# The last layer norm of a one-core decoder step: weight and offset rows in accumulator banks, the shift as a two-scalar form, and the moments of three row tiles on ScalarE

## The reference, cut to what matters

```
def _layer_norm(x, g, b):
    xf = x.astype(jnp.float32)
    mu = jnp.mean(xf, axis=-1, keepdims=True)
    var = jnp.mean(jnp.square(xf - mu), axis=-1, keepdims=True)
    return ((xf - mu) * lax.rsqrt(var + EPS) * g.astype(jnp.float32) + b.astype(jnp.float32)).astype(x.dtype)
...
        x = _layer_norm(DEEPNORM_ALPHA * x + ffn, ln2_g[l], ln2_b[l])
```

## Time and profile before

| | us |
|---|---|
| median of three runs (1813.81 to 1816.19) | 1814.46 |
| the profiled execution's own time | 1814.07 |
| its span in the trace | 1812.3 |
| last stage: first load issued | 1765.42 |
| last stage: first tile there, VectorE starts on it | 1769.18 |
| last stage: last VectorE instruction starts, 1.23 long | 1807.98 |
| last stage: last three stores (tiles 6, 7, 8) issued in a row from | 1805.75 |

### The profile page before, as it was taken

One profiled execution on the slowest core, in us unless ns is written; L12 is line 12 of the kernel. 1 busy time (PEld: TensorE's weight loads), 2 busy tenths in 40 slices (PEclk: granted clock), 3 DMA queues, 4 the chain that ended last, 5 costly groups with the idle time before them and its releaser, 6 DMA issues. The chain is left out here.

```text
span 1812.3 us, 18129 instructions
## 1 busy us (share of the span) xinstructions
PE 1639.4 (90%) x6288; PEld 993.8 (55%) x6288; DVE 526.2 (29%) x1115; ACT 394.0 (22%) x1000; POOL 301.0 (17%) x244
## 2 busy tenths in 40 slices
PE   8999999989889999999986399999999999999950
PEld 7666666656656777777763244444444444444420
DVE  1344444322153445554432500000000000000008
ACT  1211111131034444443420011111111111111102
POOL 0000000021033244443310001111111111111106
PEclk8899999988899999999996599999999999999985
DMA  6132222251343222212112479999999999999935
GB/s 238 37 97 73 75 74 77 59 163 37 110 162 120 82 89 81 94 54 81 53 40 78 161 247 322 325 325 326 321 325 325 329 317 323 326 325 326 321 79 196
DMA packets 177492, 325.83 MB, mean 180 GB/s; under 512 B 43432, under 2 KB 73048, under 8 KB 176152
## 3 DMA queue, kind: packets, MB, share of 16 engines
q1 hardware_dynamic: 166776, 294.30, 46.9%
q0 software_dynamic: 9504, 26.23, 6.2%
q10 hardware_dynamic: 1152, 4.52, 0.6%
HBM read 281.33 MB, written 52.07 MB: 184 GB/s over the span
## 5 line engine op out<-in xcount | busy, mean ns | idle before, releaser
L2075 PE MATMUL bank<-sb_arena 128*128 128x512 f32 x1024 | 451.9, 594 | 2.6 <-ACT sb_arena L2120 2.6
L377 PE MATMUL bank<-sb_arena 128*128 128x368 f32 x1056 | 331.8, 477 | 6.8 <-DMA sb_arena<-xT 6.8
L2075 PEld LDWEIGHTS bank<-sb_arena 128*128 128x128 f32 x1024 | 192.7, 191 | 233.4 <-issue 230.2
L377 PEld LDWEIGHTS bank<-sb_arena 128*128 128x128 f32 x1056 | 202.7, 192 | 133.8 <-DMA sb_arena<-w_conv 6.8
L2091 PE MATMUL bank<-sb_arena 128*128 128x512 f32 x512 | 226.9, 596 | 8.4 <-DMA sb_arena<-w 8.4
L2174 DVE TENSOR_SCALAR sb_oidx<-sb_slot 128x1 int32 x32 | 4.9, 154 | 548.5 <-DMA d_acc<-sb_arena,sb_oidx 548.4
L2091 PEld LDWEIGHTS bank<-sb_arena 128*128 128x128 f32 x512 | 95.5, 192 | 116.9 <-issue 108.2
L2048 POOL DMA_INDIRECT d_acc<-sb_arena,sb_oidx x32 | 51.0, 1592 | 609.0 <-ACT sb_arena L2138 609.0
L941 PE MATMUL bank<-sb_arena 128*128 128x512 f32 (+1 forms) x288 | 133.9, 606 | 6.3 <-DVE sb_rlog L1545 5.0
L742 PE MATMUL bank<-sb_arena 128*128 128x384 f32 (+1 forms) x288 | 100.9, 504 | 8.5 <-DVE sb_arena L1561 8.5
L2120 ACT ACTIVATE sb_arena<-bank 128x512 f32<-128x512 f32 x66 | 35.9, 596 | 266.5 <-PE bank L2069 266.5
(11 more groups left out here) (321 smaller groups left out, 1713.7 us busy)
## 6 DMA issues: line engine op xcount, KB each, us to landing
sb_arena<-w SPq DMA_DIRECT2D x192, 1024.0 KB, 7.9
sb_arena<-w_conv SPq DMA_DIRECT2D x28, 512.0 KB, 4.9
sb_arena<-d_conv SPq DMA_DIRECT2D x7, 1792.0 KB, 7.3
d_conv<-sb_arena SPq DMA_DIRECT2D x22, 512.0 KB, 3.3
sb_arena<-d_gam SPq DMA_DIRECT2D x8, 768.0 KB, 4.1
d_x<-sb_arena SPq DMA_DIRECT2D x9, 512.0 KB, 2.6
sb_arena<-xT ACTq DMA_DIRECT2D x8, 552.0 KB, 9.6
sb_arena<-w_out SPq DMA_DIRECT2D x8, 512.0 KB, 7.5
```

The costliest lines, as they stand in the source:

```text
L377: last = e.matmul(bank[3 * r + s][:, 0:TN], wring[n % NV][:, k, :], xT[:, k, TN * s:TN * s + TN], start=(k == 0), stop=(k == KT - 1))
L2075: mm = e.matmul(bank[bk][:], xgT[:, k, :], w[:, k, :], start=(k == 0), stop=(k == KT - 1))
```

## The change

The change leaves the order of tiles, the loads, the stores, `power` and `offset` on GpSimd as they are, and does three things:

1. VectorE copies `lnrow` into banks 0 to 3 (four copies of 128 x 512) at the start of the stage, in the place of a tiny `memset`, and `gain` and VectorE's own offset add read these banks, as two instructions over 512 columns each instead of one over 1024.
2. `shift` becomes a `tensor_scalar`: one tensor input, the root as a per-partition scalar and -1.0 as the second scalar.
3. For tiles 1, 4 and 7 (`BY_ACT`) the mean and variance are worked out on ScalarE by `moments(t)`: a Copy activation over the tile with an accumulated sum, a [128,1] Copy that scales the sum to minus the mean, a Square activation over the tile with that as bias and an accumulated sum, and a [128,1] Copy that scales and adds the epsilon. Each of the four waits for the one before it. ScalarE does `moments(t)` ahead of the normalisation of tile t-1. `stats` is left out for these tiles on VectorE. GpSimd's `power(t)` waits for the engine that did the tile.

```
+BY_ACT = (1, 4, 7)
...
                     e.wait_ge(S["c_rstd"], t + 1)
-                    e.scalar_tensor_tensor(rv[t][0:n, 2:3], mv2[t][0:n, 0:1], -1.0, rv[t][0:n, 1:2], ALU.mult, ALU.mult).then_inc(S["c_nmr"], 1)
+                    if t in BY_ACT:
+                        step = e.tensor_scalar(rv[t][0:n, 2:3], st[t][0:n, 0, 1:2], rv[t][0:n, 1:2], None, ALU.mult)
+                    else:
+                        step = e.tensor_scalar(rv[t][0:n, 2:3], mv2[t][0:n, 0:1], rv[t][0:n, 1:2], -1.0, ALU.mult, ALU.mult)
+                    step.then_inc(S["c_nmr"], 1)
...
-                    e.tensor_tensor(rows[t][0:n], rows[t][0:n], lnrow[0:n, 0, :], ALU.mult).then_inc(S["c_g"], 1)
+                    for s in range(2):
+                        half = rows[t][0:n, s * 512:(s + 1) * 512]
+                        last = e.tensor_tensor(half, half, bank[s][0:n, :], ALU.mult)
+                    last.then_inc(S["c_g"], 1)
                     if not by_gpsimd(t):
                         e.wait_ge(S["c_g"], t + 1)
-                        e.tensor_tensor(rows[t][0:n], rows[t][0:n], lnrow[0:n, 1, :], ALU.add).then_inc(S["c_yv"], 1)
-
-                e.memset(rv[0][0:1, 3:4], 0.0).then_inc(S["c_go"], 1)
+                        for s in range(2):
+                            half = rows[t][0:n, s * 512:(s + 1) * 512]
+                            last = e.tensor_tensor(half, half, bank[2 + s][0:n, :], ALU.add)
+                        last.then_inc(S["c_yv"], 1)
+
+                for q in range(4):
+                    last = e.tensor_copy(bank[q][:], lnrow[:, q // 2, (q % 2) * 512:(q % 2 + 1) * 512])
+                last.then_inc(S["c_ln"], 1)
+                e.wait_ge(S["c_ln"], 1)
                 for t in range(NTT + 2):
-                    if t < NTT:
+                    if t < NTT and t not in BY_ACT:
                         stats(t)
...
             @block.scalar
             def _(e):
-                for t in range(NTT):
+                def moments(t):
+                    n = m_of(t)
+                    e.wait_ge(S[f"c_in{t:02d}_"], 16)
+                    e.activation(junk[t][0][0:n], rows[t][0:n], ACT.Copy, accum_out=st[t][0:n, 0, 0:1]).then_inc(S["c_sum"], 1)
+                    e.wait_ge(S["c_sum"], nth(t))
+                    e.activation(st[t][0:n, 0, 1:2], st[t][0:n, 0, 0:1], ACT.Copy, scale=-1.0 / D).then_inc(S["c_nm"], 1)
+                    e.wait_ge(S["c_nm"], nth(t))
+                    e.activation(junk[t][1][0:n], rows[t][0:n], ACT.Square, bias=st[t][0:n, 0, 1:2], accum_out=st[t][0:n, 0, 2:3]).then_inc(S["c_sq"], 1)
+                    e.wait_ge(S["c_sq"], nth(t))
+                    e.activation(rv[t][0:n, 0:1], st[t][0:n, 0, 2:3], ACT.Copy, scale=1.0 / D, bias=EPS / ALPHA ** 2).then_inc(S[f"c_ve{t:02d}_"], 1)
+
+                def normal(t):
                     n = m_of(t)
                     e.wait_ge(S["c_nmr"], t + 1)
                     e.activation(rows[t][0:n], rows[t][0:n], ACT.Identity, bias=rv[t][0:n, 2:3], scale=rv[t][0:n, 1:2]).then_inc(S["c_xn"], 1)
+
+                for t in range(NTT + 1):
+                    if t in BY_ACT:
+                        moments(t)
+                    if t >= 1:
+                        normal(t - 1)
...
                 def power(t):
                     n = m_of(t)
-                    e.wait_ge(S["c_mve"], t + 1)
+                    if t in BY_ACT:
+                        e.wait_ge(S[f"c_ve{t:02d}_"], 1)
+                    else:
+                        e.wait_ge(S["c_mve"], nth(t))
```

More of the change, by code:

```diff
@@ L2193, in program @@
         rows = [A(P, D) for _ in range(NTT)]
+        junk = {t: [A(P, D) for _ in range(2)] for t in BY_ACT}
         st = [A(P, 2, 6) for _ in range(NTT)]
@@ L2196, in program, with nth @@
         rv = [A(P, 4) for _ in range(NTT)]
-        sem("c_go", "c_st", "c_mv", "c_mve", "c_rstd", "c_nmr", "c_xn", "c_g", "c_yp", "c_yv", "c_out")
-        sem(*[f"c_in{t:02d}_" for t in range(NTT)])
+        sem("c_ln", "c_st", "c_mv", "c_mve", "c_sum", "c_nm", "c_sq", "c_rstd", "c_nmr", "c_xn", "c_g", "c_yp", "c_yv", "c_out")
+        sem(*[f"c_in{t:02d}_" for t in range(NTT)], *[f"c_ve{t:02d}_" for t in BY_ACT])
         def by_gpsimd(t):
             return t < NTT - 2
+        def nth(t):
+            return len([u for u in range(t + 1) if (u in BY_ACT) == (t in BY_ACT)])
         begin()
@@ L2226, in stats @@
                     last.then_inc(S["c_st"], 1)
-                    e.wait_ge(S["c_go"], 1)
-                    e.wait_ge(S["c_st"], t + 1)
+                    e.wait_ge(S["c_st"], nth(t))
                     e.bn_aggr(mv2[t][0:n], st[t][0:n].rearrange("p a b -> p (a b)")).then_inc(S["c_mv"], 1)
-                    e.wait_ge(S["c_mv"], t + 1)
+                    e.wait_ge(S["c_mv"], nth(t))
                     e.tensor_scalar(rv[t][0:n, 0:1], mv2[t][0:n, 1:2], EPS / ALPHA ** 2, None, ALU.add).then_inc(S["c_mve"], 1)
```

## The result

The changed kernel takes 1804.64 us (median of five, 1804.39 to 1805.84) against 1814.46 before (five runs, where the table ahead says three; 1813.81 to 1816.19): a ratio of 0.9946, 95% interval 0.9931 to 0.9960, so 0.54% faster. The forecast was 1806, range 1803 to 1810.5.

A forecast was written before the change was run, and what follows sets the result against it. VectorE and GpSimd shutting each other out was taken to bound the last stage. VectorE ending at 1798.96 and three crowded stores put its end at 1803.7, 8.6 us sooner: 1805.5, with the median's 0.4 forecast as 1806, range 1803 to 1810.5.

The forecast's parts named there:

- What bounds the kernel now: Last stage: VectorE instructions with two SBUF inputs and GpSimd's tensor_tensor shut each other out; a shift takes 3.93 us.
- Weight and offset rows in banks: Gain as two halves of 0.69 us, 1.31 in all, its and power's waits gone; four copies, 2.5 us, beside the load.
- The shift as a `tensor_scalar`: VectorE's [128,1] shift: 0.15 us, not held by GpSimd; other bound up to 2.3 us for each tile.
- Moments on ScalarE: Tiles 1, 4, 7: 2.95 us each, bounds 2.6 to 4.0, no table load; worth nothing in the sum.
- The rival in which GpSimd holds the new shift: Shift still waits for GpSimd's offset; stage ends at 1802.9, time about 1808; chance 0.10.
- The rival in which ScalarE is the bound: Each us on the moments moves the end by 3; at 4.0 us time 1808.5; chance 0.12.
- The layout: Last stage laid out step by step with the forecast durations; for the kernel before it ends at 1808.5, trace 1809.21.
- The sum: Last chain: ScalarE's last moments end at 1790.06, GpSimd's offset of tile 3 at 1790.22, VectorE at 1798.96.
- The stores: Tiles 6, 7 and 8 stored almost together: 1798.2 + 0.8 + 3 x 1.3 + 0.8 = 1803.7; one alone 1802.1.
- The slower-side rival: Bank operands don't lift the lockout, both gain halves held by GpSimd: time 1814.8; lockout stays, chance 0.06.
- The time: Whole program: 1805.5 us from the profiled execution's 1814.07, median 0.4 above it, so 1806.

The follow-up runs named there:

- e3: Changed kernel without moments on ScalarE and with the old shift with two SBUF inputs; 1804.26 us, ratio 0.9946.
- e11: Changed kernel with gain and VectorE's offset add in halves read from SBUF rows, not banks, and no moments on ScalarE; 1809.84 us, ratio 0.9983.
- e5: Changed kernel with gain and VectorE's offset add still in halves but read from SBUF rows, not banks, moments kept; 1810.13 us, ratio 0.9982.
- e1: Changed kernel with all moments back on VectorE (BY_ACT empty); 1804.45 us, ratio 0.9949.
- e4: Changed kernel with only the new shift: gain and offset read SBUF, 1024 wide, no moments on ScalarE; 1813.13 us, ratio 0.9995.
- e8: Changed kernel with a second, unused Square activation in each of the three moments; 1807.85 us, ratio 0.9970.
- e6: Changed kernel with SyncE storing tile 7 before tile 6; 1804.38 us, ratio 0.9952.
- e9: Changed kernel with GpSimd doing offset(t-2) instead of offset(t-3) behind power(t); 1802.39 us, ratio 0.9941.

## Why the prediction was right, point by point

- *What bounds the kernel now.* Shown. An instruction of VectorE with two SBUF inputs and GpSimd's `tensor_tensor` shut each other out, and this sets the pace: with the second input in a bank the stage is 9.7 us shorter than before (e3), with the same halves from SBUF 2.2 (e11) or, with the moments, 4.1 (e5). The cleanest pair is e11 and e1, with nothing but that input between them: 7.1 us.
- *Weight and offset rows in banks.* Right, and the whole of the gain: e3 has nothing else bar the halves, which come with this form, as each bank tensor is 512 wide. The halves have a share of their own, some 2.6 of the 9.7 us (e4 against e11), for which the prediction had no term. The halves were priced at 0.69 and took 0.68; the four copies took 2.47 us against 2.5 and lay beside the load.
- *The shift as a `tensor_scalar`.* Not held, as forecast, but 0.21 us, not 0.15, so the per-partition scalar costs 0.05. The rival in which GpSimd holds the new shift is ruled out. What the prediction didn't see is that the old form is hardly held either, once the gains are free (e3), and that the new form is worth nothing alone (e4). Beside the banks the new form brings VectorE's end forward by 1.0 us (e1 against e3), and the crowded stores give that back. The 3.93 us that I showed first was a consequence.
- *Moments on ScalarE.* 2.89 us from the first activation at 1769.32 to the variance at 1772.21, against 2.95; no table load in the stage. That they are worth nothing in the changed kernel is shown by e1. The rival in which ScalarE is the bound was priced rightly, as e8 shows: a slope of 3 against some 2.8 measured, and for moments of 4.0 us an end 32.9 us after the first stats and a time of 1808.5, where moments of 3.93 gave 32.3 and 1807.85. One step was off: the prediction had three of them in the last chain, where there were two. The third ended at 1788.72, while GpSimd's offset ended at 1789.04, so the chain kept to GpSimd from 1780.54 on. The layout had 1790.06 against 1790.22, a tie of this very kind, and the prose took the wrong side of it. It moved no number, for the layout itself went on from GpSimd's 1790.22.
- *The sum.* VectorE's end, counted from its first stats, was laid out as 29.8 us (1769.15 to 1798.96) and is 29.2. Of the 0.6, 0.4 is tile 1, there at 1769.32, 0.88 after tile 0 and not 1.28; from there to VectorE's end the layout had 28.5 us and the trace has 28.3.
- *The stores.* Right: issue of tile 6 to the end was to be 5.5 us and was 5.7 (1797.0 to 1802.7). e6 and e9 show that it is the crowding of the three: the tail goes from 5.1 to 4.0 and to 3.1 when their order or spacing is changed.
- *The slower-side rival.* With banks its mechanism didn't come, and its price was wrong: with SBUF operands, halves, new shift and moments together (e5) the time is 1810.1, not 1814.8. It had both halves of a gain held by GpSimd, which in e5 happens to one pair, and it gave no credit for power waiting for a half only (0.82 us on average in e5, 1.31 before).
- *The time.* 1806 forecast, 1804.6 measured, 1.4 less. The stage came out right to 0.1 us, and that is in part luck, for three errors cancel: from the first load to the first stats 4.0 us and not 3.7, from there to VectorE's end 29.2 and not 29.8, from there to the span's end 5.1 and not 4.7. Of the 1.4, 1.0 lies ahead of the stage, 0.3 in the median, which stood only 0.1 above the profiled execution and not 0.4, and the rest in rounding.

## What to carry to other kernels

When a [128,1] instruction takes 4 us, look at what the engine that shuts it out is running meanwhile, and free the long instructions first: one operand in an accumulator bank did it, while changing the short one that showed the wait only moved the wait on. Taking work off the busiest engine pays only if the path that it opens elsewhere is shorter: the moments took 4 us off VectorE and put as much on the way through ScalarE and GpSimd, so the end did not move. And after compute gets shorter, look at when the last outputs become ready: by the profiles 2 of the 11 us saved went into three stores behind each other, and one small edit (the offset one tile sooner) gave them back.

## What the runs showed of the hardware that I had not expected

- The lockout is taken instruction by instruction: splitting a gain of 1.21 us into halves of 0.68, both from SBUF, shortened GpSimd's power from 1.30 to 0.96 us on average and VectorE's part of the stage by 2.9 us (e4 against e11), though the halves are in sum longer. The Trainium skill (SBUF — State Buffer, SBUF: two separate sides) says that the loser is kept out for the whole instruction of the other; the traces agree: each half of the pair shown for e5 ends some 0.55 us after an offset of GpSimd does.
- The one shut out can be passed over more than once. In the kernel before, the shift of 3.93 us stood through the rest of one offset, a power and another offset of GpSimd; in e4 a whole gain of 4.95 us from 1781.33 did the same. In other places the engines take turns, as in the pair of e5 above. What decides between the two isn't shown.
- A `tensor_scalar` on [128,1] takes 0.15 us with constants (L2235) and 0.21 with a per-partition scalar (L2243).
